# Decoder layer with 32 experts: the down weights of each expert issued by ScalarE instead of SyncE

## What is computed

```python
def moe_ffn(h, w_router, b_router, w_gate_up, b_gate_up, w_down, b_down):
    ...
    top_vals, top_idx = lax.top_k(logits, TOP_K)      # 4 of 32 experts for each token
    gate = jax.nn.softmax(top_vals, axis=-1)
    ...
    def expert_block(args):
        xb, e = args
        hgu = xb @ w_gate_up[e] + b_gate_up[e]        # 1024 x 2048
        return clamped_swiglu(hgu) @ w_down[e] + b_down[e]    # 1024 x 1024
```

## Time and profile before

| | |
|---|---|
| Median of 3 runs | 1223.66 us (1222.31 to 1224.81) |
| The profiled execution, its own time | 1226.88 us |
| its span, first to last instruction | 1225.1 us |
| TensorE busy | 93% of the span |
| VectorE, ScalarE busy | 20%, 13% |
| Mean granted TensorE clock | 0.956 of full |
| Bytes moved | 426.76 MB, 348 GB/s over the span |
| Chain that ended last | DMA 54%, PE 41%, ACT 2%, DVE 2% |

### The profile page before, as it was taken

One profiled execution on the slowest core, in us unless ns is written; L12 is line 12 of the kernel. 1 busy time (PEld: TensorE's weight loads), 2 busy tenths in 40 slices (PEclk: granted clock), 3 DMA queues, 4 the chain that ended last, 5 costly groups with the idle time before them and its releaser, 6 DMA issues.

```text
span 1225.1 us, 13679 instructions
## 1 busy us (share of the span) xinstructions
PE 1140.0 (93%) x5564; PEld 533.6 (44%) x5564; DVE 246.0 (20%) x565; ACT 163.8 (13%) x340; POOL 15.4 (1%) x39
## 2 busy tenths in 40 slices
PE   7989789989999999999999999999999999999997
PEld 3555566564444444333333333333333333333332
DVE  2322354121111122111111111111111111111111
ACT  1322441121110011000000000000000000000001
POOL 4000000000000000000000000000000000000000
PEclk9988856978999999999999999999999999999999
DMA  9952400238999999999999999999999999999997
GB/s 219 359 194 75 162 1 1 77 112 338 418 418 419 417 418 418 417 418 418 417 418 418 418 418 417 419 418 417 419 418 417 419 418 417 417 418 418 418 417 280
DMA packets 82464, 426.76 MB, mean 348 GB/s; under 512 B 3657, under 2 KB 8865, under 8 KB 49649
## 3 DMA queue, kind: packets, MB, share of 16 engines
q1 hardware_dynamic: 81664, 424.85, 85.6%
q0 software_dynamic: 784, 1.71, 1.3%
HBM read 425.49 MB, written 1.05 MB: 348 GB/s over the span
## 4 chain that ended last, share of the span: by engine, by line
DMA 54%; PE 41%; ACT 2%; DVE 2%; issue 1%; SPq 0%; POOL 0%; DVEq 0%; POOLq 0%
DMA stage<-in_w_gate_up 51%; PE bank L1371 15%; PE bank L1072 7%; PE bank L1380 4%; PE bank L1361 3%; PE bank L1283 2%; DMA stage<-in_w_down 2%; PE bank L1117 1%; PE bank L1403 1%; PE bank L1094 1%; PE bank L1083 1%; PE bank L1108 1%; PE bank L1259 0%; PE bank L1395 0%; PE bank L1243 0%
## 5 line engine op out<-in xcount | busy, mean ns | idle before, releaser
L1371 PE MATMUL bank<-stage,xs 128*64 128x512 f32 x2048 | 460.5, 599 | 48.3 <-DMA stage<-in_w_gate_up 47.0
L1371 PEld LDWEIGHTS bank<-stage,xs 128*64 128x64 f32 x2048 | 141.2, 137 | 363.1 <-issue 272.2
L1380 PE MATMUL bank<-stage,actf 128*64 128x512 f32 x1024 | 227.0, 595 | 1.2 <-DMA stage<-in_w_down 1.2
L1361 PEld LDWEIGHTS bank<-onehot,h2n 128*128 128x128 f32 x1024 | 120.0, 196 | 26.4 <-issue 26.4
L1380 PEld LDWEIGHTS bank<-stage,actf 128*64 128x64 f32 x1024 | 70.6, 137 | 132.4 <-issue 121.4
L1361 PE MATMUL bank<-onehot,h2n 128*128 128x64 f32 x1024 | 124.4, 281 | 1.2 <-DVE onehot L685 1.2
L993 DVE COPY gu<-bank 128x512 f32<-128x512 f32 x32 | 22.1, 691 | 449.7 <-PE bank L1371 449.7
L1072 PE MATMUL bank<-stage,xt 128*128 128x512 f32 (+2 forms) x224 | 89.1, 560 | 0.8 <-DVE xt L694 0.8
L613 ACT COPY gu<-bank 128x512 f32<-128x512 f32 x32 | 18.8, 586 | 490.1 <-PE bank L1371 490.1
L1015 DVE TENSOR_TENSOR pgr<-iota_f,posm 128x256 f32<-128x256 f32 x32 | 13.6, 425 | 315.3 <-PE bank L1388 315.3
L1403 PE MATMUL bank<-ys,pgt 64*128 64x512 f32 x256 | 63.6, 615 | 1.0 <-ACT ys L617 1.0
(11 more groups left out here) (292 smaller groups left out, 525.8 us busy)
## 6 DMA issues: line engine op xcount, KB each, us to landing
stage<-in_w_gate_up SPq DMA_DIRECT2D x128, 2048.0 KB, 23.9
stage<-in_w_down SPq DMA_DIRECT2D x62, 2048.0 KB, 24.0
stage<-in_w_in SPq DMA_DIRECT2D x4, 2048.0 KB, 23.4
stage<-in_w_out SPq DMA_DIRECT2D x2, 2048.0 KB, 14.5
stage<-in_w_down SPq DMA_DIRECT2D x4, 1024.0 KB, 18.5
stage<-in_w_in SPq DMA_DIRECT2D x1, 2112.0 KB, 23.7
stage<-in_cmp_w_k SPq DMA_DIRECT2D x1, 2048.0 KB, 21.7
stage<-in_cmp_w_v SPq DMA_DIRECT2D x1, 2048.0 KB, 22.4
```

What stands on the lines that cost most here:

```text
L1361: last = mm(x_bank[:, k * CAP:(k + 1) * CAP], h2n[:, ti, k * P:(k + 1) * P], onehot[:, ti, :], start=ti == 0, stop=ti == NT - 1)
L1371: last = mm(up_banks[a][b * CAP:(b + 1) * CAP, :], xs[:, k, :], w[:, kk, FF * a + 512 * b:FF * a + 512 * (b + 1)], start=k == 0, stop=k == ...
L1380: last = mm(down_bank[b * CAP:(b + 1) * CAP, :], actf[:, kk, j, :], w[:, kk, 512 * b:512 * (b + 1)], start=j == 0 and kk == 0, stop=j == D ...
```

## The change

SP's `fetch` calls for the pieces 4 and 5 (down 0 and down 1) are gone from its loop and from the step behind it. ACT gets a function `fetch_down`, which waits for the buffer and issues the transfer on ACT's own queue. It is called once ahead of the loop, behind `gate_of(0)`, for expert 0, and in each step directly behind `down_out`, for the expert `it`. The up pieces and the four halves at the end stay with SP.

```diff
@@ -327,16 +327,14 @@
             with sp.Fori(1, last_step) as it:
                 this = sp.snap(it % E, min_val=0, max_val=E - 1)
-                before = sp.snap((it + (E - 1)) % E, min_val=0, max_val=E - 1)
                 after = sp.snap((it + 1) % E, min_val=0, max_val=E - 1)
-                for j in range(NSLOT - UP_PIECES, PIECES):
-                    fetch(it, j, this if j < UP_PIECES else before)
+                for j in range(NSLOT - UP_PIECES, UP_PIECES):
+                    fetch(it, j, this)
                 for j in range(NSLOT - UP_PIECES):
                     fetch(it, j, after)
             this = sp.snap(last_step % E, min_val=0, max_val=E - 1)
-            before = sp.snap((last_step + (E - 1)) % E, min_val=0, max_val=E - 1)
-            for j in range(NSLOT - UP_PIECES, PIECES):
-                fetch(last_step, j, this if j < UP_PIECES else before)
+            for j in range(NSLOT - UP_PIECES, UP_PIECES):
+                fetch(last_step, j, this)
@@ -630,12 +628,21 @@
             gate_of(0)
+
+            def fetch_down(expert, uses):
+                for j in range(UP_PIECES, PIECES):
+                    i = body_slot(j)
+                    act.wait_ge(s[f"used{i}"], uses)
+                    act.dma_start(piece_of(i, j), expert_source(expert, j)).then_inc(s[f"stage{i}"], 16)
+
+            fetch_down(0, 1)
             act.wait_ge(s["rounds"], 1)
             last_step = act.value_load(rounds_i[0:1, 0:1], min_val=E - 1, max_val=ROUNDS * E - 1)
             with act.Fori(1, last_step) as it:
                 glu_out(body_slot(UP_PIECES - 1), it + 1)
                 rows_in(it + 1)
                 down_out(body_slot(PIECES - 1), it + 1)
+                fetch_down(act.snap(it % E, min_val=0, max_val=E - 1), it + 1)
                 slots_out(it - 1)
                 gate_of(it)
```

## The result

| | before | after |
|---|---|---|
| Median (4 runs each, beside each other) | 1224.24 us | 1241.89 us |
| Ratio, 95% interval | | 1.0145, 1.012 to 1.017 |
| Span of the profiled execution | 1225.1 us | 1240.3 us |
| Mean granted clock | 0.956 | 0.944 |

The forecast was +11.5 us, 1227 to 1240; it came to +17.65 in the medians and +15.2 between the profiled spans. The gap between the two is in the profiled execution of before: at 1226.88 us it was 2.6 us above its median, that of after (1242.09) 0.2 above. The clock in the table is the granted TensorE clock as a share of full.

A forecast was written before the change was run, and what follows sets the result against it. The prediction took one unbroken 418 GB/s weight stream as the bound, with PE nearly a second. Start +4.4, order of landing +8.3 and end -1.2 gave +11.5 us: 1223.66 to 1235.2 us, range 1227 to 1240.

The forecast's parts named there:

- The bound and its reading: From 300 us on, one unbroken 418 GB/s weight stream bounds; time moves only at its early standstill, rate or last pieces' order.
- Rival D: Steady stream: two queues fill the engines better, 433 instead of 418 GB/s, time about 1204 us; chance 0.08.
- rival B: Queue order: ScalarE's pieces go behind what SyncE's queue was already given, only the start is paid, +4.4, 1228.1 us; chance 0.14.
- Step 1: SyncE's loop: two waits and two issues fewer per expert, its longest issue should disappear; worth 0.
- Step 2: ScalarE between its two copies: two issues cost PE 0.6 us an expert, absorbed by its 1.93 us wait; cost 0.
- Step 3: Start: first down pieces issued at 291.5 us behind ScalarE's first sigmoid, stream stands still, delay reaches its end; +4.4 us.
- Step 4: Steady loop: both queues share bytes equally, up pieces land later, PE runs 8.3 us later behind the stream, paid once.
- rival A: Both queues share by packets, up pieces get twice the bytes, PE waits for down weights; +12.5 to +13.5 us; chance 0.22.
- the lag: PE's distance behind the stream, forecast to grow by 1.65 pieces, 8.3 us, and be paid once when the stream ends.
- Since it never again runs dry: Stream after the start: no later standstill as before, same bytes, so the whole 4.4 us delay reaches its end.
- Step 5: End: PE's chain behind the last up piece loses its 1.20 us wait for down 1; -1.2, sum +11.5 us.
- rival C: PE becomes the bound through dearer ScalarE issues or half clock after lumped waits; 15 us on top, 1250 us; chance 0.10.

The follow-up runs named there:

- e10: Kernel before, one queue, with SyncE issuing the first two down pieces only after ScalarE's first sigmoid; +4.6 us against before, ratio 1.0044.
- e3: Kernel after, with ScalarE issuing down 0 in the loop ahead of its copy of the down products, when its buffer is free; +13.3 us against before, ratio 1.0087.
- e9: Kernel after with three edits: expert 0's down pieces issued early, down 0 at its buffer's release, expert 30's down pieces on SyncE; +8.3 us against before, ratio 1.007.
- e2: Kernel after, with the down pieces of expert 30, the loop's last, issued by SyncE behind the last up pieces; +20.2 us against before, ratio 1.0166.
- e1: Kernel after, with ScalarE issuing expert 0's down weights directly behind glu_out, ahead of rows_in(1) and the first sigmoid; +15.6 us against before, ratio 1.0118.

## Why the prediction was wrong

- **The bound and its reading** (one stream, the time can move at its start, its rate or its end) was right, as far as it went. The rate did not move: 418 GB/s in the slices without a dip. Rival D is out. So is rival B, the order kept: down 0 lands 11.4 us after its issue and not 24.
- **Step 1, SyncE's share:** right. Its issues are 0.37 us each now and the long ones are gone; nothing came of it. (The longest in before was 5.6 us and not the 4.89 that I called so.)
- **Step 2, ScalarE's issues:** right in size. Two take 0.94 us, the combine waits 0.5 us per expert (15.6 in all), and the run with small transfers shows PE's slack taking most of such a wait (9.5 us more there, 7.2 less for up weights). The run with four issues shows what it costs beyond the slack.
- **Step 3, the start, +4.4:** right, by the windows, by e10 (+4.6, stream +5.2), and by e3, whose stream has that alone (+4.6).
- **Step 4, the order of landing:** the share failed, and with it the size. I took equal shares because "nothing in the rows prefers a queue", though my own rows 9 counted packets of 4 KB and rival A had the condition. While both queues have work rows go 1 to 1, bytes 2 to 1. The Trainium skill (DMA: Bandwidth & Descriptors, Queues, rings and completion order) says that a DMA engine takes turns between its queues packet by packet. The trace agrees as far as it counts: rows of 8 and 4 KB come 280 to 281, rows of 4 and 4 KB 417 to 417; how many rows one turn takes no run here shows. With 2 to 1 PE waits for down weights and has all up weights at hand, so what limits it is not what the sum had. The 8.2 us above are not the 8.3 of the sum: that one was counted at the products on the last up 3. There before has 18.2 us of stream left (1212.9 less 1194.65), after 12.5 (it comes to up 3 at about 1210.3, three quarters into its last up block). So in the sum's own terms the lag is **5.7 us, not 8.3**.
- **The sentence that cost most:** "Since it never again runs dry", and with it that the steady part costs nothing "while both queues together hold work". They did not: this is the step that failed. I had named no place in the steady part where they could be empty: behind a late down 1, with four up buffers full and down 0's free but not yet issued. That is **5.5 us of dips, put at nothing**, no term of the sum and in no rival. The signs were there: the change issues down 0 behind a wait for down 1, 3.5 us after its buffer is free.
- **Step 5, the end:** the sum took off 1.2 us, the wait for down 1; that wait only shrank to 0.67, and from up 3 to the span's end after needs 30.0 us instead of 30.45, -0.5. So the forecast's 4.4 + 8.3 - 1.2 = 11.5 was 4.4 + 5.5 + 5.7 - 0.5 = 15.1 for the spans, 15.2 as measured. A lag taken 2.6 us too long hid half of the missing dips: that the forecast came as near as it did is in part luck.
- **The parts by the runs:** start +5.2 (e10), dips 5.4 (stream of after less that of e3), lag 5.8 (e9) make 16.4 for the 15.3 to the end; in the medians 4.6 + 4.4 + 8.3 = 17.3 for 17.7. Each is known to some 3 us only.
- **Rival A** named the mechanism and undersized it: 12.5 to 13.5 us. Its end (down 1 lands last of all) is not what happened, as e2 shows. The clock that falls behind long waits, which stands under rival C, came in: down products take 18 us more in all (245.3 against 227.0), and PE is busy 9.5 us longer (1149.5 against 1140.0). No run holds the clock up on two queues, so what the half clock adds to the time, as part of the lag above all, was not measured by itself.

What stays open is how the lag divides between the shares and the clock, and why the dips fall where they do. They change with small shifts of the start (e1), so a single profile does not give their sum for the next kernel.

## What to carry to other kernels

When a stream on one queue is split, the consumer's order of landing is given up, and while both queues have work bytes are shared by the length of the rows (shown for 8 and 4 KB, and for 4 and 4 KB), not by need: count how far the pieces of each queue may come late, and what is empty when they do. A buffer should be issued again at its own release; two that are issued together behind the second turn one late piece into a pause of the stream. If the stream is the bound, look for what holds it at its start, here PE's clock, before touching who issues it.

## What the runs showed of the hardware

- ScalarE's issue of a 2 MB transfer takes 0.39 us in the median (at most 0.80), like SyncE's 0.37. With two transfers of 2 KB rows for each piece the medians were 0.39 and 0.58 us, single ones took up to 2.2.
- With work on both queues rows go 1 to 1: 280 to 281 packets of 8 and 4 KB, 417 to 417 of 4 and 4 KB.
- Rows of 8 KB beside rows of 4 KB stream at 418 GB/s, all rows at 4 KB at 410: 22 us here. I had expected less than 9.
- Two transfers of 64-byte rows per step lowered the stream from 418 to 416 GB/s, 4 us for 0.5 MB.
- The granted clock fell to 0.50 before the end of a wait of 4.7 us (1.00 up to 346, 0.50 from 347 us, PE starts at 347.45), and held at 1.00 through those of 0.6 and 1.3 us. With 19 products of 256 columns in PE's waits it stayed at 1.00 from 245 to 300 us, where before it was at 0.50 from 251.5 to 268 and again from about 289 to 295.
